# Two experts' token rows in one indirect transfer, with a list's ranks spread over the partitions

## What is computed

```python
for e in range(N_EXPERTS):                      # 32 experts, each token has 2 of them
    h = jax.nn.silu(x2d @ w_gate[e]) * (x2d @ w_up[e])      # 1024 -> 256
    y = y + combine[:, e:e + 1] * (h @ w_down[e])           # 256 -> 1024
```

## Time and profile before

| | |
|---|---|
| median of 3 runs | 1363.9 us (1361.18 to 1366.36) |
| the profiled execution, its own time | 1367.46 us |
| its span | 1365.7 us, 24555 instructions |
| TensorE busy | 1248.9 us (91% of the span) |
| VectorE / ScalarE / GpSimd busy | 549.3 / 491.4 / 180.0 us |
| DMA moved | 197.64 MB, mean 145 GB/s |
| the experts | from 484.7 us (first load after the barrier) to 733 us (last expert's output) |
| rows back, residual and norm | to about 762 us |

### The profile page before, as it was taken

One profiled execution on the slowest core, in us unless ns is written; L12 is line 12 of the kernel. 1 busy time (PEld: TensorE's weight loads), 2 busy tenths in 40 slices (PEclk: granted clock), 3 DMA queues, 4 the chain that ended last, 5 costly groups with the idle time before them and its releaser, 6 DMA issues. The chain is left out here.

```text
span 1365.7 us, 24555 instructions
## 1 busy us (share of the span) xinstructions
PE 1248.9 (91%) x10411; PEld 974.0 (71%) x10411; DVE 549.3 (40%) x973; ACT 491.4 (36%) x859; POOL 180.0 (13%) x239
## 2 busy tenths in 40 slices
PE   6999999999989759998794599999999999999988
PEld 5787765699858535564352498888886677888888
DVE  3434553435372313332123523344446773553241
ACT  4224547512253301111011424455556663332230
POOL 4000013100000022222111001122210014400000
PEclk9999999999999869998987699999999999999999
DMA  4422100000129799999997353632216117212031
GB/s 155 131 93 62 32 1 0 10 4 4 52 69 381 264 321 386 384 366 384 389 409 276 86 149 117 110 93 93 93 32 93 63 33 274 67 62 93 1 108 47
DMA packets 93112, 197.64 MB, mean 145 GB/s; under 512 B 10134, under 2 KB 73708, under 8 KB 80076
## 3 DMA queue, kind: packets, MB, share of 16 engines
q1 hardware_dynamic: 87228, 185.57, 40.1%
q0 software_dynamic: 5200, 8.40, 1.9%
q10 hardware_dynamic: 576, 2.10, 0.4%
HBM read 185.79 MB, written 17.86 MB: 149 GB/s over the span
## 5 line engine op out<-in xcount | busy, mean ns | idle before, releaser
L1929 PE MATMUL hidden_ps<-w_gate,gathered_t 128*64 128x256 f32 x384 | 94.5, 402 | 0.0
L1929 PE MATMUL hidden_ps<-w_up,gathered_t 128*64 128x256 f32 x384 | 94.5, 403 | 0.0
L649 DVE TENSOR_TENSOR w_in_low<-w_in_raw,w_in_high 128x2048 fp32r<-128x2048 f32 x20 | 45.9, 2293 | 116.4 <-ACT w_in_high L641 116.4
L601 PE MATMUL proj_ps<-block_in_high,w_in_low 128*128 128x512 f32 x232 | 90.7, 391 | 0.0
L601 PE MATMUL proj_ps<-block_in_low,w_in_high 128*128 128x512 f32 x232 | 90.6, 391 | 0.0
L601 PE MATMUL proj_ps<-block_in_high,w_in_high 128*128 128x512 f32 x232 | 90.5, 390 | 0.0
L1475 PE MATMUL wo_ps<-w_out_high,wo_x_high 128*128 128x256 f32 x256 | 74.8, 292 | 3.5 <-DVE w_out_low L660 3.5
L2769 PE MATMUL gate_ps<-block_in_high,gate_w_high 128*128 128x512 f32 x192 | 76.0, 396 | 1.0 <-PEq L2438 1.0
L2769 PE MATMUL gate_ps<-block_in_low,gate_w_high 128*128 128x512 f32 x192 | 75.0, 391 | 0.0
L2769 PE MATMUL gate_ps<-block_in_high,gate_w_low 128*128 128x512 f32 x192 | 74.9, 390 | 0.0
L1929 PEld LDWEIGHTS hidden_ps<-w_gate,gathered_t 128*64 128x64 f32 x384 | 53.5, 145 | 29.6 <-issue 5.7
(11 more groups left out here) (474 smaller groups left out, 3125.5 us busy)
## 6 DMA issues: line engine op xcount, KB each, us to landing
w_down<-exp_w_down_dram SPq DMA_DIRECT2D x27, 1024.0 KB, 28.7
w_gate<-exp_w_gate_dram SPq DMA_DIRECT2D x24, 1024.0 KB, 23.5
w_up<-exp_w_up_dram SPq DMA_DIRECT2D x24, 1024.0 KB, 27.9
w_in_raw<-w_in_dram SPq DMA_DIRECT2D x20, 1024.0 KB, 5.7
slot_scratch_and_keys<-w_in_dram SPq DMA_DIRECT2D x14, 1024.0 KB, 5.4
vb<-w_in_dram SPq DMA_DIRECT2D x6, 1024.0 KB, 5.7
gate_w_raw_odd<-w_in_dram SPq DMA_DIRECT2D x6, 1024.0 KB, 6.2
slot_scratch_and_keys<-exp_w_down_dram SPq DMA_DIRECT2D x5, 1024.0 KB, 28.7
```

The costliest lines, as they stand in the source:

```text
L601: m = pe.matmul(out, a(k)[i], b(k)[j], start=(k == 0 and i + j == 0), stop=(k == n - 1 and i == 1))
L649: dve.tensor_tensor(self.part[1][n % 2], self.slot(n), self.part[0][n % 2], ALU.subtract).then_inc(self.low, 1)
L1929: x = pe.matmul(g_bank[e % 2][a * CAP:(a + 1) * CAP, 0:DE], xT[e % 2][:, k, :], w[:, k, :], start=(k == 0), stop=(k == KC - 1))
```

## The change

One indirect transfer serves two experts. A pair's rows stand on all 128 partitions of one tile: the even expert on 0 to 63, the odd one on 64 to 127, as they did before. There are 17 gathers in place of 33 and 16 scatters in place of 32, each over 128 rows; the rows that carry data are the same 1024 and 1024. The waits are counted in pairs: gather `i` waits until both experts of pair `i-2` have been turned, a scatter until both experts' outputs are stored. The number of tiles stays: `GB` = `YB` = 2 pairs, and `LAG` is 3 pairs.

`Lists.product` writes the even experts' places to partitions 0 to 63 of the bank and the odd experts' to 64 to 127: 16 matmuls of 32 columns in place of 8 of 64. `list_places` becomes 128 x 16 x 2.

`place_row` is filled by 4 iotas in place of one. It still holds each of 0 to 63 once, in another order: ranks 0 to 31 stand on every second partition of a half, the even ones on even partitions of one group of 16 and the odd ones on odd partitions of the next, and ranks 32 to 63 stand in between.

```diff
+NP = NE // 2
-GB, YB = 4, 4
-LAG = 6
+GB, YB = 2, 2
+LAG = 3
...
-        pool.iota(self.M["place_row"][:, :], [[1, CAP]], base=0, channel_multiplier=0, allow_small_or_imprecise_dtypes=True).then_inc(self.made, 1)
+        ranks = self.M["place_row"][:, :].rearrange("p (a z n b) -> p a z n b", a=2, z=2, b=2)
+        for odd in range(2):
+            for z in range(2):
+                pool.iota(ranks[:, :, z, :, odd], [[CAP // 4, 2], [2, CAP // 8]], base=odd + (z != odd) * CAP // 2, channel_multiplier=0,
+                          allow_small_or_imprecise_dtypes=True).then_inc(self.made, 1)
...
     def product(self, pe, n, at, bank):
         for jc in range(2 * TT):
-            x = pe.matmul(bank[0:CAP, 0:2 * NE], at[:, jc, :], self.M["marks"][:, jc, :, :].rearrange("p a e -> p (a e)"),
-                          start=(jc == 0), stop=(jc == 2 * TT - 1))
+            marks = self.M["marks"][:, jc, :, :].rearrange("p a (i b) -> p b a i", b=2)
+            for odd in range(2):
+                x = pe.matmul(bank[odd * CAP:(odd + 1) * CAP, 0:NE], at[:, jc, :], marks[:, odd, :, :],
+                              start=(jc == 0), stop=(jc == 2 * TT - 1))
...
-    def gather(self, pool, e):
-        pool.indirect_dma_start(out=self.xg[e % GB], out_offset=None, in_=self.M["xn_dram"],
-                                in_offset=bass.IndirectOffsetOnAxis(ap=self.idx[:, e, 0:1], axis=0),
-                                bounds_check=S - 1, oob_is_err=False).then_inc(self.x_in[e % GB], 16)
+    def gather(self, pool, i):
+        pool.indirect_dma_start(out=self.pairs[i % GB][:, :], out_offset=None, in_=self.M["xn_dram"],
+                                in_offset=bass.IndirectOffsetOnAxis(ap=self.idx[:, i, 0:1], axis=0),
+                                bounds_check=S - 1, oob_is_err=False).then_inc(self.x_in[i % GB], 16)
...
-                    for i in range(1, NE + LAG):
-                        if i < NE:
+                    for i in range(1, NP + LAG):
+                        if i < NP:
                             if i >= GB:
-                                pool.wait_ge(turned, rnd * NE + i - GB + 1)
+                                pool.wait_ge(turned, rnd * NE + 2 * (i - GB) + 2)
                                 pool.sem_inc(seen)
                             lists.gather(pool, i)
-                        e = i - LAG
-                        if e >= 0:
-
-                            pool.wait_ge(y_lo, rnd * NE + e + 3)
-                            pool.wait_ge(y_hi, rnd * NE + e + 3)
+                        j = i - LAG
+                        if j >= 0:
+
+                            pool.wait_ge(y_lo, rnd * NE + 2 * j + 4)
+                            pool.wait_ge(y_hi, rnd * NE + 2 * j + 4)
                             pool.sem_inc(seen)
-                            write_rows(idx[:, e, 1:2], e)
+                            write_rows(idx[:, j, 1:2], j)
```

More of the change, by code:

```diff
@@ L1537 @@
 class Router:
-    MADE = 8
+    MADE = 11
     def __init__(self, s, A, M, const, h, room, spare):
@@ L1731, in __init__ @@
         self.M = M
[L1732 to L1736, removed]
+        self.idx = s.sb_right("list_places", [P, NP, 2], I32)
+        self.offs, self.placed = s.sb_right("place_offsets", [P, 2, NP]), s.sb_right("placed", [P, 2, NP])
+        self.pairs = [s.sb_right(f"gathered{j}", [P, D]) for j in range(GB)]
         self.marked, self.less, self.listed, self.shifted, self.ready = (
@@ L1758, in store @@
         dve.wait_ge(self.offs_made, 1)
-        dve.tensor_tensor(self.placed[:, :, :], bank[0:CAP, 0:2 * NE].rearrange("p (a e) -> p a e", a=2), self.offs[:, :, :],
+        dve.tensor_tensor(self.placed[:, :, :], bank[:, 0:NE].rearrange("p (a i) -> p a i", a=2), self.offs[:, :, :],
                           ALU.add).then_inc(self.shifted, 1)
         dve.wait_ge(self.shifted, n + 1)
-        dve.tensor_copy(self.idx[:, :, :].rearrange("p e a -> p a e"), self.placed[:, :, :]).then_inc(self.ready, 1)
-    def gather(self, pool, e):
-        pool.indirect_dma_start(out=self.xg[e % GB], out_offset=None, in_=self.M["xn_dram"],
-                                in_offset=bass.IndirectOffsetOnAxis(ap=self.idx[:, e, 0:1], axis=0),
-                                bounds_check=S - 1, oob_is_err=False).then_inc(self.x_in[e % GB], 16)
+        dve.tensor_copy(self.idx[:, :, :].rearrange("p i a -> p a i"), self.placed[:, :, :]).then_inc(self.ready, 1)
+    def gather(self, pool, i):
+        pool.indirect_dma_start(out=self.pairs[i % GB][:, :], out_offset=None, in_=self.M["xn_dram"],
+                                in_offset=bass.IndirectOffsetOnAxis(ap=self.idx[:, i, 0:1], axis=0),
+                                bounds_check=S - 1, oob_is_err=False).then_inc(self.x_in[i % GB], 16)
     def first_gather(self, pool):
-        pool.iota(self.offs[:, :, :], [[S, 2], [0, NE]], base=S, channel_multiplier=0, allow_small_or_imprecise_dtypes=True).then_inc(self.offs_made, 1)
+        pool.iota(self.offs[:, :, :], [[S, 2], [0, NP]], base=S, channel_multiplier=0, allow_small_or_imprecise_dtypes=True).then_inc(self.offs_made, 1)
         for pair in self.pairs:
             pool.memset(pair[:, :], 0.0).then_inc(self.zeroed, 1)
-        pool.wait_ge(self.zeroed, GB // 2)
+        pool.wait_ge(self.zeroed, GB)
         pool.wait_ge(self.M["xn_in"], 16 * TT)
@@ L1799, in experts @@
         lists = M["lists"]
-        idx, xg, x_in = lists.idx, lists.xg, lists.x_in
+        idx, pairs, x_in = lists.idx, lists.pairs, lists.x_in
         wg.append(s.sb("w_gate7", [P, KC, DE]))
@@ L1810, in experts @@
         hid = [s.sb(f"hidden{j}", [P, FC, CAP]) for j in range(2)]
-        y_pairs = [s.sb(f"expert_out{j}", [P, D]) for j in range(YB // 2)]
-        y = [y_pairs[j // 2][j % 2 * CAP:(j % 2 + 1) * CAP, :] for j in range(YB)]
+        y_pairs = [s.sb(f"expert_out{j}", [P, D]) for j in range(YB)]
+        y = [y_pairs[j // 2][j % 2 * CAP:(j % 2 + 1) * CAP, :] for j in range(2 * YB)]
         t_bank = [s.ps(f"gathered_ps{j}") for j in range(2)]
@@ L1834, in experts, with uses @@
         squared, gsquared, fin, root = s.sem("fin_squares"), s.sem("fin_gained_squares"), s.sem("fin_step"), s.sem("fin_root")
-        def uses(rnd, e, n):
-            return rnd * len(range(e % n, NE, n)) + e // n
+        def uses(rnd, e, n, of=NE):
+            return rnd * len(range(e % n, of, n)) + e // n
         def rounds(eng):
@@ L1880, in _, with write_rows @@
             def _(pool):
-                def write_rows(places, e):
+                def write_rows(places, i):
                     return pool.indirect_dma_start(out=y_dram, out_offset=bass.IndirectOffsetOnAxis(ap=places, axis=0),
-                                                   in_=y[e % YB], in_offset=None, bounds_check=2 * S - 1,
-                                                   oob_is_err=False).then_inc(y_out[e % YB], 16)
+                                                   in_=y_pairs[i % YB][:, :], in_offset=None, bounds_check=2 * S - 1,
+                                                   oob_is_err=False).then_inc(y_out[i % YB], 16)
                 pool.sem_inc(places_free)
@@ L1909, in _ @@
                     lists.gather(pool, 0)
-                pool.wait_ge(x_in[0], last * (16 * len(range(0, NE, GB))) + 16)
+                pool.wait_ge(x_in[0], last * (16 * len(range(0, NP, GB))) + 16)
             @block.tensor
@@ L1915, in turn_tokens @@
                 def turn_tokens(rnd, e):
-                    pe.wait_ge(x_in[e % GB], uses(rnd, e, GB) * 16 + 16)
+                    i, at_half = e // 2, slice(e % 2 * CAP, (e % 2 + 1) * CAP)
+                    pe.wait_ge(x_in[i % GB], uses(rnd, i, GB, NP) * 16 + 16)
                     pe.sem_inc(seen_pe)
-                    cols, at_half = xg[e % GB].rearrange("c (p k) -> c k p", k=KC), slice(e % 2 * CAP, (e % 2 + 1) * CAP)
+                    cols = pairs[i % GB][at_half, :].rearrange("c (p k) -> c k p", k=KC)
                     for k in range(KC):
@@ L1973, in store_high @@
                     act.wait_ge(y_r, rnd * NE + e + 1)
-                    if e >= YB:
-                        act.wait_ge(y_out[e % YB], uses(rnd, e, YB) * 16)
-                    act.activation(y[e % YB][:, 512:D], y_bank[e % 2][CAP:P, :], ACT.Copy).then_inc(y_hi, 1)
+                    if e >= 2 * YB:
+                        act.wait_ge(y_out[e // 2 % YB], uses(rnd, e // 2, YB, NP) * 16)
+                    act.activation(y[e % (2 * YB)][:, 512:D], y_bank[e % 2][CAP:P, :], ACT.Copy).then_inc(y_hi, 1)
                 with act.Fori(0, rounds(act)) as rnd:
@@ L2017, in store_low @@
                     dve.wait_ge(y_r, rnd * NE + e + 1)
-                    if e >= YB:
-                        dve.wait_ge(y_out[e % YB], uses(rnd, e, YB) * 16)
-                    dve.tensor_copy(y[e % YB][:, 0:512], y_bank[e % 2][0:CAP, :]).then_inc(y_lo, 1)
+                    if e >= 2 * YB:
+                        dve.wait_ge(y_out[e // 2 % YB], uses(rnd, e // 2, YB, NP) * 16)
```

(1 more changed line is left out.)

2 lines of the change are left out of this document (1 added, 1 removed).

## The result

The changed kernel takes **1344.7 us** in the median of 4 runs (1339.3 to 1350.8), against 1362.5 of 4 runs of the kernel before beside it. The ratio is 0.985, with a 95% interval of 0.982 to 0.989: 15 to 25 us are gone. A second set of 6 runs (experiment 5) gives 0.988 (0.985 to 0.991). I had predicted 1355, with a range of 1346 to 1366.

The account below looks back on a forecast made before the run. The prediction took the weights' DMA stream to bound the experts' stage; -10.5 (gathers' excess) + 0.3 (product) + 0.6 (issue) + 0.4 (last scatter) = -9.2 us, against 1363.9 giving 1355, range 1346 to 1366.

Parts of the forecast that it names:

- What bounds the kernel: Experts' stretch: the weights' stream bounds it at DMA share 1.01 or 1.02; TensorE catches up at about 620 us.
- The size of what could come back: Experts' weight stream, 490 to 698 us: 20.5 us missing against 422 GB/s over 31 gathers, 0.66 us each.
- The share of it that comes back: Gathers: 9.6 us through half rate on 64 partitions, plus 1 us of the unassigned 10.9: -10.5, ends 0 and -20.5.
- count, unevenness and row reads: Possible causes of the unassigned 0.35 us per gather: number of transfers (5 us back), uneven DMA engines (part), single-row DRAM reads (nothing).
- the gathers' excess that comes back: Term for stream time that gathers cost beyond their bytes in the experts' stretch: -10.5 us.
- Rival 2: Experts' stretch: all 20.5 us come back, +1.3 of additions, 1345 us; needs partitions, count and unevenness as whole cause; chance 0.12.
- The product of the lists: Before the barrier: 16 products of half width in place of 8; between nothing and +1.97 us, taken as +0.3.
- Issue: GpSimd's issue of 128 rows: +0.3 us ahead of the barrier and again at the last scatter, +0.6 in all.
- The last scatter: Stage's end: it now carries experts 30 and 31, so its rows land later; +0.4 us, upper end 3.1.
- The wait of 7.64 us: TensorE's wait for expert 1's rows at the start goes, worth nothing since the stream covers it.
- The signs: Profile after: some 400 GB/s, q0 4752 packets, 7.64 us wait gone, last output about 9 us earlier, TensorE waiting before 618.
- rival 3: Stage's serial ends grow and the stream gains nothing: +5 to +7 us, 1369 to 1371; chance 0.08.

Follow-up runs that it names:

- experiment 5: The changed kernel again, unaltered, as base for two further variants: 1348.6 us, ratio 0.988 to the kernel before.
- Experiment 3: Kernel before with expert 1's gather issued ahead of the barrier, behind expert 0's: 1361.3 us, ratio 0.999, stage 248.2 us.
- experiment 9: Kernel before with only the gathers of experts 0 to 3 left, the others working on wrong tokens: 1334.7 us, ratio 0.979, stage 221.1 us.
- experiment 6: Changed kernel with gathers still paired but scatters again one per expert out of 64 partitions: 1343.6 us, ratio 0.984, stage 227.8 us.
- experiment 4: Changed kernel with one gather per expert over all 128 partitions, other half's rows empty, LAG 2: 1348.5 us, ratio 0.988.
- experiment 2: Kernel before with the new order of ranks alone, still 64 rows per transfer: 1362.9 us, ratio 0.9996, stage 248.0 us.
- Experiment 1: Changed kernel with the old plain order of ranks (one iota), pairs kept: 1347.6 us, ratio 0.988, stage 228.6 us.
- experiment 8: Kernel before with each gathered row cut to 2 KB, same 33 transfers into 64 partitions, wrong data: 1342.5 us, ratio 0.986, stage 232.7 us.

## Why the prediction was wrong, and where it was right

**What bounds the kernel: right.** The weights' stream bounds the stage. Experiment 3 takes out a wait of TensorE and gains nothing; every kernel here with a faster stream is faster.

**The size of what could come back: right.** I had 20.5 us, 0.66 per gather, from windows of one profile. Measured: 22.05 us of the stage, 0.71 per gather, and 0.70 in experiment 9. Also right: scatters cost their bytes only, which I had from two windows and experiment 6 shows.

**The share of it that comes back: the step that failed.** "That explains 0.31 of the 0.66 us, or 31 x 0.31 = 9.6 us. With both halves in one transfer it goes. The other 0.35 us per gather (10.9 us) I can't assign." I took 10.5 us; all of the loss went. Half of full rate for half of the partitions was a model, and I let it set the size of the cause as well as its kind. What it left over I handed to count, unevenness and row reads. The runs give these nothing: count 0 (experiment 4), unevenness nothing in the time of the kernel before and at most 1.4 us at the end of the paired one (experiments 2 and 1), row reads 0, since the paired kernel reads the same rows at 418 GB/s. A gather's 131 KB cost 0.31 us of bytes and 0.70 us of loss, together 1.0 us: as long as its bytes alone at some 130 GB/s, a third of the full rate, with nothing beside them. The term that was mis-sized is the gathers' excess that comes back: -10.5 predicted, -22.05 measured by the stage. Had I put the unassigned part where the assigned one was, the sum would have been -19.2 and the time 1345.

I had a row that should have led me there: from 490 to 498 us, "where no engine's queue can have run dry, the excess is there already". I used it against unevenness, and still held 1 us for it and shared the rest among causes of which each had less for it than the span of partitions. Rival 2 had 0.12; "it needs partitions, count and unevenness to be the whole cause" was wrong, it needed partitions alone.

The Trainium skill (SBUF — State Buffer, "Door 1: The DMA port swizzle") offers a cause in kind, ports that depend on a transfer's partitions, and its two figures (196 against 328 GB/s, 1.7 times) would leave even less than my half. It gives them at 1 MB, and no run here has a narrow transfer of that size; beside a full stream a gather costs three times its bytes here. The Trainium skill (DMA: Bandwidth & Descriptors, "Rules for kernel authors") advises one transfer over 128 partitions in place of two over the halves. Experiment 1 agrees; experiment 4 shows that here two transfers do as well, if each spans all 128. No run here shows which DMA engine writes which partitions, nor what happens at a port, so why it is a third stays open.

**The product of the lists:** +0.3 predicted, nothing measured (1.92 us for 1.97): twice the matmuls of half the width take no longer, so the halves overlap. **Issue:** +0.3 twice predicted, 1.22 for 1.14 us at the first and 0.97 for 0.89 at the last: +0.08 each. From the product's start to the first load it is 9.21 us, before 8.88: +0.33, where I had +0.6 with the product. **The last scatter:** +0.4 predicted, 6.78 for 6.39 us: +0.4. Behind it comes what I had not seen: VectorE's four additions of rows, without a gap in the earlier trace rows, now have one of 1.18 us, because a part of the rows lands later. From the last scatter to the next block's first load it is 31.5 us, before 29.8: +1.7 in all, which comes off the stage's 22.

**The wait of 7.64 us: right.** It is gone, and it was worth nothing: experiment 3. The few us that I expected pair 1 to be late by didn't come: TensorE's longest gap from 486 to 640 us is 1.03 us, and it waits for no rows.

**The signs.** q0's packets: right. GB/s "up to some 400": too low, the same failure. "The last expert's output about 9 us before 733": its copy starts at 708.4 and not 732.4, so 24 us, of which 1.9 are the stage's earlier start. "TensorE waiting for weights sooner than 618 us": wrong. Its first gap over 0.5 us behind 500 us ends at 649.13, where the kernel before has one of 3.17 us that ends at 626.28. I had counted its earlier start and not the faster stream: at 418 GB/s an expert's weights and rows (3.15 + 0.26 MB) take 8.15 us, at 378 they take 9.0, so TensorE, with 6.5 us, catches up more slowly.

**Slower (rival 3): its mechanism is there and small.** The ends grew by 0.3 and 1.7 us.

## What to carry to other kernels

When DMA bounds a stage, look at GB/s at a full share, not at the share: here 375 and 418 both stood beside 1.02. An indirect transfer that wrote 64 of 128 partitions beside a full stream cost far more than its bytes, so give it all 128, if need be with empty rows; one that read 64 of them didn't. A plain load of 64 partitions beside such a stream wasn't tried. And where rows give the whole size of an effect but a model explains only half of it, let the likeliest cause have the rest too, or widen the range to where it would.

## What the runs showed that I had not expected

- A gather of 131 KB into 64 partitions takes 0.70 us of a stream of 418 GB/s beyond its own 0.31 us, and half as much with half of the bytes, which are then half of the packets too (experiments 8 and 9). Over 128 partitions it takes none that can be seen, even with one half empty (experiment 4).
- Empty rows are nearly free for the stream: 2448 more packets in experiment 4 for 1 to 3 GB/s. On GpSimd an indirect transfer of 128 rows costs 1.00 to 1.02 us in the median, one of 64 rows 0.89 to 0.94.
- The stream held 416 to 424 GB/s on this core for over 200 us. The Trainium skill (DMA: Bandwidth & Descriptors, "Specifications") gives about 358 for HBM per core, which it works out as half of what two cores share; with one core at work these traces don't show that limit.
- Single runs of one kernel differ by up to 14 us. In the profiles the part behind the next block's first load takes 598 to 599 us where the clock is 0.91 to 0.93 in its first 30 us, and 602 to 604 us where it is 0.78 to 0.80. A profile pair that straddles this shows 4 to 6 us that no change made.
